# Forming the final row with tokens on partitions, in a one-layer decoder step

## The reference

```python
def rms_norm(x, g):
    return x * lax.rsqrt(jnp.mean(x * x, axis=-1, keepdims=True) + EPS) * g

def conv_ffn(h, buf, w_up, conv_w, conv_b, w_down):
    a, b = jnp.split(jnp.einsum('btd,de->bte', h, w_up), 2, axis=-1)
    a_ext = jnp.concatenate([buf, a], axis=1)
    c = conv_b + sum(conv_w[j] * a_ext[:, j:j + T] for j in range(3))
    y = jax.nn.gelu(c) * b
    return jnp.einsum('btf,fd->btd', y, w_down), a_ext[:, T:]

h = rms_norm(x, p['g_pre_ffn'])
y, new_buf = conv_ffn(h, conv_buf, p['w_up'], p['conv_w'], p['conv_b'], p['w_down'])
x = x + rms_norm(y, p['g_post_ffn'])
```

## Time and profile before

| | us |
|---|---|
| median of 3 runs | 2733.76 |
| lowest, highest run | 2732.91, 2734.69 |
| span of the profiled execution | 2732.5 |
| PE busy | 2686.0 |
| DVE busy | 1602.1 |
| ACT busy | 1075.3 |
| GpSimd (POOL) busy | 207.7 |

### The profile page before, as it was taken

One profiled execution on the slowest core, in us unless ns is written; L12 is line 12 of the kernel. 1 busy time (PEld: TensorE's weight loads), 2 busy tenths in 40 slices (PEclk: granted clock), 3 DMA queues, 4 the chain that ended last, 5 costly groups with the idle time before them and its releaser, 6 DMA issues.

```text
span 2732.5 us, 49450 instructions
## 1 busy us (share of the span) xinstructions
PE 2686.0 (98%) x20118; PEld 2555.5 (94%) x20118; DVE 1602.1 (59%) x2383; ACT 1075.3 (39%) x1357; POOL 207.7 (8%) x295
## 2 busy tenths in 40 slices
PE   8999999999999999999999999999999999999998
PEld 7999887899999999999989969999999999999997
DVE  5564564476777767777546334485655555653334
ACT  5333445444444444444333234342332233343324
POOL 0102311111111111111100000000000000000000
PEclk9999999999999999999999999999999999999999
DMA  9746656765555556555464694555555555555554
GB/s 268 206 124 164 214 169 209 225 192 157 155 141 159 154 149 163 141 159 154 132 200 130 223 385 110 144 167 149 154 146 146 153 150 144 142 139 150 153 151 146
DMA packets 693464, 458.69 MB, mean 168 GB/s; under 512 B 13646, under 2 KB 661422, under 8 KB 687342
## 3 DMA queue, kind: packets, MB, share of 16 engines
q1 hardware_dynamic: 681008, 414.25, 53.8%
q0 software_dynamic: 8608, 28.06, 3.6%
q10 hardware_dynamic: 3712, 14.35, 1.4%
HBM read 429.91 MB, written 26.72 MB: 167 GB/s over the span
## 4 chain that ended last, share of the span: by engine, by line
PE 93%; DVE 3%; DMA 2%; ACT 1%; issue 0%; SPq 0%; POOL 0%; DVEq 0%; ACTq 0%
PE psum L596 20%; PE psum L601 20%; PE psum L598 20%; PE psum L852 4%; PE psum L1284 4%; PE psum L1285 4%; PE psum L1286 4%; PE psum L857 2%; PE psum L994 1%; PE psum L997 1%; PE psum L990 1%; DMA ring<-in_w_in 1%; PE psum L1165 1%; PE psum L710 1%; PE psum L1006 1%; PE psum L1044 1%
## 5 line engine op out<-in xcount | busy, mean ns | idle before, releaser
L596 PE MATMUL psum<-x_high,w_high 128*128 128x320 f32 x3808 | 1123.8, 311 | 0.5 <-ACT w_high L2022 0.5
L598 PE MATMUL psum<-h_low,w_high 128*128 128x320 f32 x3312 | 974.3, 309 | 0.0
L1331 DVE TENSOR_TENSOR w_low<-ring,w_high 128x2048 fp32r<-128x2048 f32 x292 | 676.1, 2315 | 312.8 <-ACT w_high L2022 312.4
L2022 ACT ACTIVATE w_high<-ring 128x2048 fp32r<-128x2048 f32 x294 | 561.6, 1911 | 678.2 <-PE psum L601 554.9
L596 PEld LDWEIGHTS psum<-x_high,w_high 128*128 128x128 f32 x3808 | 713.0, 188 | 5.8 <-issue 2.4
L598 PEld LDWEIGHTS psum<-h_low,w_high 128*128 128x128 f32 x3312 | 621.9, 188 | 1.6
L601 PE MATMUL psum<-x_high,w_low 128*128 128x320 f32 x3808 | 597.4, 309 | 0.0
L601 PEld LDWEIGHTS psum<-x_high,w_low 128*128 128x128 f32 x3808 | 568.5, 188 | 0.0
L1284 PE MATMUL psum<-y_high,w_down_high 128*128 128x320 f32 x704 | 217.8, 309 | 1.2 <-DVE w_low L1941 1.2
L1286 PE MATMUL psum<-y_high,w_low 128*128 128x320 f32 x704 | 216.3, 307 | 0.0
L1285 PE MATMUL psum<-y_low,w_down_high 128*128 128x320 f32 x704 | 216.2, 307 | 0.0
(11 more groups left out here) (424 smaller groups left out, 2840.9 us busy)
## 6 DMA issues: line engine op xcount, KB each, us to landing
ring<-in_w_in SPq DMA_DIRECT2D x128, 1024.0 KB, 5.8
ring<-in_w_up SPq DMA_DIRECT2D x88, 1024.0 KB, 5.8
ring<-in_w_down SPq DMA_DIRECT2D x64, 704.0 KB, 4.8
ring<-in_w_xk SPq DMA_DIRECT2D x16, 1024.0 KB, 5.7
ring<-in_w_xv SPq DMA_DIRECT2D x16, 1024.0 KB, 5.0
ring<-in_w_out SPq DMA_DIRECT2D x16, 1024.0 KB, 6.0
ring<-in_w_xq SPq DMA_DIRECT2D x16, 1024.0 KB, 6.2
ring<-in_w_xo SPq DMA_DIRECT2D x16, 1024.0 KB, 6.0
```

The costliest lines, as they stand in the source:

```text
L596: mm(out, w_hi[:, j % 2, k, :], x_hi[:, k, :], start=k == 0, stop=False)
L598: mm(out, w_hi[:, j % 2, k, :], lo[:, k, :], start=False, stop=False)
L1331: V.tensor_tensor(w_lo[:, j], ring[:, j], w_hi[:, j % 2].bitcast(FP32), ALU.subtract).then_inc(N.slab_lo, 1)
L2022: F(w_hi[:, j % 2], ring[:, j], ACT.Copy).then_inc(N.slab_hi, 1)
```

## The change

- **x is turned early.** After each of the first two calls of `conv_gate`, DVE turns two chunks of x, all 32x32 blocks at once (`x_rows_turned`, four transposes of 128x1280), into the still empty end of `yT`. When all four are done ACT issues four DMAs that write x to DRAM as rows of tokens, in runs of 32 numbers (128 bytes), 5120 runs each. The parking by line 2686 goes. DVE waits for the four DMAs before its pass 6.
- **The convolution's columns** are turned by DVE in two transposes of 128x704 after two tiles of the down-projection; 16 GpSimd DMAs send them at once, in runs of 128 bytes. PE's and ACT's 11 groups in the tail go.
- **The tail.** SP fetches x as rows. PE turns the raw scaled `hT` without waiting for the root, three of twelve pieces ahead of the sums; the sums put one number per token on its partition (eight products with one column), so the root is 128x3. DVE does eight pieces in one operation each, h times root plus x, out of PSUM; ACT scales the four sample pieces and GpSimd adds them. ACT sends `y_sample` in one DMA.

```diff
...
             sp.wait_ge(N.slab_used, B_DOWN + R * (KD - 1) + 1)
-            sp.dma_start(xT, xt_dram).then_inc(N.x_fetched, 16)
-            sp.wait_ge(N.cn_evac, 11)
...
+            sp.wait_ge(N.x_parked, 16 * 4)
+            sp.dma_start(x_prompt, xr_dram[0:SEQ].rearrange("(m p) d -> p m d", p=P)).then_inc(N.x_fetched, 16)
+            sp.dma_start(x_sample, xr_dram[SEQ:T]).then_inc(N.x_fetched, 16)
             for q in range(4):
...
+                sp.wait_ge(N.xo_edve, 2 * q + 2)
+                sp.dma_start(O["y_prompt"][0].rearrange("(m p) d -> p m d", p=P)[:, :, c], x_prompt[:, :, c])\
                   .then_inc(N.final_sent, 16)
...
+            for u in range(3):
+                rows_out(u)
             pe.wait_ge(N.n_sum, 3)
...
+            pe.wait_ge(N.n_t, KD)
+            for b in (1, 2):
+                for m, r0, r1 in ((0, 0, P), (1, 0, P), (2, 0, NS), (2, NS, P)):
+                    t0 = TOK[m][0]
+                    last = mm(bank(b)[r0:r1, m:m + 1], sqacc[:, t0:t0 + r1 - r0], ones[:, 0:1], start=True, stop=True)
+                last.then_inc(N.n_mm, 1)
+            for u in range(3, 12):
+                rows_out(u)
...
+            def x_rows_turned(q):
+                dve.wait_ge(N.n_x, 8)
+                V.transpose(x_turned[:, q], chunk(xT, q)).then_inc(N.x_turned, 1)
...
             conv_gate(0, 0, False, first=(4,))
+            x_rows_turned(0)
+            x_rows_turned(1)
             conv_gate(0, 1, False, 6, 7, first=(5,))
+            x_rows_turned(2)
+            x_rows_turned(3)
...
             y_low(0, slice(0, DOWN_K))
+            dve.wait_ge(N.x_parked, 16 * 4)
             gates(6, FT // 2 - 7)
...
+            for half in range(2):
+                V.transpose(conv_turned[half], conv_window(half)).then_inc(N.conv_T, 1)
...
-            for q in range(4):
-                dve.wait_ge(N.n_t, 4 * q + 4)
-                st.then(V.tensor_tensor(chunk(hT, q), chunk(hT, q), bcast(rstd, 4), ALU.mult))
-                V.tensor_tensor(chunk(xT, q), chunk(xT, q), chunk(hT, q), ALU.add).then_inc(N.n_x, 1)
...
+            for u in OUT_DVE:
+                q, m = OUT_UNITS[u]
+                dve.wait_ge(N.xo_T, u + 1)
+                y = x_prompt[:, m, q * 512:(q + 1) * 512]
+                V.scalar_tensor_tensor(y, bank(OUT_BANKS[u % 6]), tok_root[:, m:m + 1], y, ALU.mult, ALU.add)\
+                    .then_inc(N.xo_edve, 1)
...
             conv_input(0, 1, False)
+            for i in range(4):
+                act.wait_ge(N.x_turned, 4)
+                act.dma_start(xr_dram.rearrange("(b t) (k i d) -> i t k b d", t=32, i=4, d=32)[i],
+                              x_turned[32 * i:32 * i + 32].rearrange("p q x -> p (q x)")
+                              .rearrange("p (k b d) -> p k b d", k=KD, d=32)).then_inc(N.x_parked, 16)
...
             inputs(1, 6)
-            act.wait_ge(N.x_parked, 16)
+            act.wait_ge(N.x_turned, 4)
...
+            for i, u in enumerate(OUT_ACT):
+                act.wait_ge(N.xo_T, u + 1)
+                F(y_part[:, i], bank(OUT_BANKS[u % 6])[0:NS], ACT.Copy, scale=tok_root[0:NS, 2:3]).then_inc(N.xo_eact, 1)
+            act.wait_ge(N.xo_pool, 4)
+            act.dma_start(O["y_sample"].rearrange("b t d -> (b t) d"), x_sample).then_inc(N.final_sent, 16)
...
-            pool.wait_ge(N.h_low, 2 * KD)
-            pool.wait_ge(N.n_sq, 10)
-            pool.dma_start(xt_dram, xT).then_inc(N.x_parked, 16)
...
+                for i in range(4):
+                    pool.dma_start(conv_prompt[i][:, f], conv_turned[half][32 * i:32 * i + 2]).then_inc(N.out_sent, 16)
+                    pool.dma_start(conv_sample[i][:, f], conv_turned[half][32 * i + 2:32 * i + 18]).then_inc(N.out_sent, 16)
+            pool.wait_ge(N.x_fetched, 32)
+            for i in range(4):
+                pool.wait_ge(N.xo_eact, i + 1)
+                y = x_sample[:, i * 512:(i + 1) * 512]
+                G.tensor_tensor(y, y, y_part[:, i], ALU.add).then_inc(N.xo_pool, 1)
```

More of the change, by code:

```diff
@@ L173, in hybrid_layer @@
         xt_dram = nc.dram_tensor("x_transposed", (P, KD, T), FP32, kind="Internal").ap()
+        xr_dram = nc.dram_tensor("x_rows_saved", (T, D), FP32, kind="Internal").ap()
         xh_dram = nc.dram_tensor("x_high_saved", (P, KD, T), FP32, kind="Internal").ap()
@@ L384, in hybrid_layer, with conv_window @@
         pcf = take(2, 4)
-        x_out = conv_rows
         assert top[0] <= SPLIT_AT
         top[0] = BASE
-        y_rows = take(3, D)
+        x_sample = take(D)[0:NS]
+        y_part = take(4, 512)[0:NS]
+        x_prompt = arena[:, X_AT:X_AT + 2 * D].rearrange("p (m d) -> p m d", m=2)
+        x_turned = yT[:, FT - KD:FT].rearrange("p k t -> p (k t)").rearrange("p (q x) -> p q x", q=4)
+        tok_root, tok_half, tok_tmp = small[:, 16:19], small[:, 24:27], small[:, 32:35]
+        def conv_window(half):
+            return bass.AP(tensor=conv_all.tensor, offset=conv_all.offset + half * (FT // 2) * 18,
+                           ap=[conv_all.ap[0], [18, FT // 2], [1, 32]])
         S = {n: sem(n) for n in """
@@ L445, in hybrid_layer @@
         Y_CUT, Y_PARTS = 6, (1, 2, 4, 5)
-        OUT_BANKS = (6, 7, 3, 0)
+        OUT_BANKS = (3, 4, 5, 6, 7, 0)
+        OUT_UNITS = [(q, m) for q in range(3) for m in range(3)] + [(3, 2), (3, 0), (3, 1)]
+        OUT_DVE = [u for u, (q, m) in enumerate(OUT_UNITS) if m < 2]
+        OUT_ACT = [u for u, (q, m) in enumerate(OUT_UNITS) if m == 2]
         ATT_S = float(P) ** -0.5
@@ L1288, in _, with rows_out @@
                         last.then_inc(N.slab_used, 1)
-            pe.wait_ge(N.n_sum, 3)
[L1290 to L1307, removed]
+            def rows_out(u):
+                q, m = OUT_UNITS[u]
+                t0, rows = TOK[m]
+                pe.wait_ge(N.n_t, 4 * q + 4)
+                if u == 5:
+                    pe.wait_ge(N.bank_free, B_DOWN + KD - 1 + FREE)
+                if u >= 6 and u - 6 in OUT_DVE:
+                    pe.wait_ge(N.xo_edve, OUT_DVE.index(u - 6) + 1)
+                elif u >= 6:
+                    pe.wait_ge(N.xo_eact, OUT_ACT.index(u - 6) + 1)
+                for c in range(4):
+                    last = tr(bank(OUT_BANKS[u % 6])[0:rows, c * P:(c + 1) * P], hT[:, 4 * q + c, t0:t0 + rows], ident)
+                last.then_inc(N.xo_T, 1)
+            for u in range(3):
+                rows_out(u)
+            pe.wait_ge(N.n_sum, 3)
+            pe.wait_ge(N.n_t, KD)
[6 more added lines that the diff above has]
+                rows_out(u)
         @block.vector
@@ L1960, in down_tile @@
                     down_low(it, e, j)
-                if not last:
-                    down_low(it, e + 1, 0)
+                if last:
+                    dve.wait_ge(N.n_sq, 11)
+                    V.tensor_tensor(sqacc, sqacc, sqbuf[:, 1], ALU.add).then_inc(N.n_sum, 1)
+                    return
+                down_low(it, e + 1, 0)
                 y = hT[:, ds(it * 2 + e, 1)].rearrange("p o t -> p (o t)")
@@ L2542, in down_tile @@
                 met()
+                if last:
+                    F(sqbuf[:, 1], bank(e)[:, 0:T], ACT.Square).then_inc(N.n_sq, 1)
+                    F(hT[:, KD - 1], bank(e)[:, 0:T], ACT.Copy, scale=G_POST_FFN[:, KD - 1:KD]).then_inc(N.n_t, 1)
+                    return
                 F(hT[:, ds(it * 2 + e, 1)].rearrange("p o t -> p (o t)"), bank(e)[:, 0:T], ACT.Copy).then_inc(N.bank_free, 1)
@@ L2551, in _ @@
             down_tile(KD // 2 - 1, 1, True)
[L2552 to L2562, removed]
+            act.wait_ge(N.n_mm, 7)
+            st.then(F(tok_root, bank(1)[:, 0:3], ACT.Ln, scale=1.0 / D, bias=small[:, 63:64]))
+            F(tok_root, tok_root, ACT.Exp, scale=-0.5).then_inc(N.n_seed, 1)
+            act.wait_ge(N.n_var, 6)
+            for i, u in enumerate(OUT_ACT):
[3 more added lines that the diff above has]
+            act.dma_start(O["y_sample"].rearrange("b t d -> (b t) d"), x_sample).then_inc(N.final_sent, 16)
         @block.gpsimd
@@ L2694, in _ @@
                                   conv_old[:, f, :].rearrange("p o (b t) -> p (o b) t", t=2)).then_inc(N.ctx_ready, 1)
-            pool.wait_ge(N.out_sent, 96)
+            conv_prompt = O["new_conv_prompt"][0, 0].rearrange("c (f i d) -> i c f d", i=4, d=32)
+            conv_sample = O["new_conv_sample"][0].rearrange("b j (f i d) -> i (b j) f d", i=4, d=32)
+            for half in range(2):
+                f = slice(half * (FT // 2), (half + 1) * (FT // 2))
+                pool.wait_ge(N.conv_T, half + 2)
+                for i in range(4):
[6 more added lines that the diff above has]
+                G.tensor_tensor(y, y, y_part[:, i], ALU.add).then_inc(N.xo_pool, 1)
+            pool.wait_ge(N.out_sent, 96 + 16 * 16)
             pool.wait_ge(N.state_sent, 32 * NHG)
```

36 lines of the change are left out of this document (18 added, 18 removed).

## The result

After the change the kernel takes 2749.09 us (median of 4 runs, 2748.18 to 2751.44), beside 2733.34 us of the kernel before, run beside it (4 runs). The ratio is 1.0056, with a 95% interval of 1.0044 to 1.0068: slower by 15.8 us, where +18.1 was forecast. The profiled execution has a span of 2747.6 us, 15.1 more than before. All medians and ratios here leave out two executions of the kernel before, run beside the last experiments, that took 3281 and 4905 us at a mean granted clock of 0.75 and 0.82.

The account below looks back on a forecast made before the run. PE was taken as the bound, busy 2686.0 of 2732.5 us. Terms -9.6 + 24.9 + 2.8 = +18.1 us gave a span of 2750.6, a median (1.3 above) of 2751.9 us; range 2729 to 2772.

Parts of the forecast that it names:

- PE's idle time at tile 6: Start of the up-projection: PE waits from 1820.65 to 1845.5 us for ACT's `w_high`, 24.9 us.
- the hold: ACT's queue before `w_high` of tile 6: four DMA issues keep ACT from 1821.0 to 1843.5 us, three behind another DMA.
- The clock: Tile 6 after PE's idle time: granted clock falls to 0.50, 24 products take 6.2 instead of 3.4 us, cost 2.8 us.
- The tail: From the last product to the end: the new tail gives 9.6 us, bounds 7.5 to 11.5.
- The eight products with one column: Sums of squares in the tail: no row shows one, taken as 1.5 us, nearer the upper bound of 2.1.
- Covered work: `w_low` of tile 5 ready 0.5 us before PE wants it; convolution columns' DMAs and transposes run beside the down-projection.
- Cost: nothing: Down-projection: the convolution columns' 16 DMAs and two transposes cost nothing there, 1.8 us if that cover is gone.
- Short issues: ACT's queue takes four large DMAs at 0.4 us each, PE idles 4.0 us: 2728.2 or 2731.0 us; chance 0.20.
- Dear writes of 28 to 50 ns: Short DRAM writes at that time a packet: ACT held 26.9 to 48 us, total 2761 to 2783 us; chance 0.15.
- Hidden: Start of tile 6: PE's wait is hidden after all, the whole 9.6 us stays, 2724.2 us; chance 0.05.
- Transposes at half rate: DVE's four transposes of x take twice 1.41 us each: 5.6 us later, 2757.5 us; no chance of its own, inside the range.
- about 3: Hold of ACT in all, in us, at which the forecast decides between faster and slower.

Follow-up runs that it names:

- the room of 32: The changed kernel with 32 instead of 24 words of room behind the saved convolution columns: 2748.03 us, ratio 1.0054 to the kernel before.

## Why the prediction was right

The sign, the mechanism and its place were right: 2751.9 us forecast, 2749.1 measured. Step by step:

- **PE's idle time at tile 6**: 24.9 us forecast, 20.5 measured. The transposes ended as forecast (1820.95 against 1821.1), and with them the wait that is left without DMAs (2.6 us). The term that was mis-sized is the hold, 22.5 us (0.4 + 1.2 + 17.3 + 3.6) against 17.87. I took 18 ns a packet, 17.3 us for three DMAs; from 1825.65 to 1839.02 us 15231 packets passed on 16 engines, 14.0 ns each, 13.4 us. The 1.2 us to the first packet and the 3.6 us of the weight load were two terms of the sum; measured, they are one stretch of 3.8 us before the first packet, in which 1819 of the load's packets passed. With 0.7 for the first issue that makes 17.9. Where the DMAs stood apart the first packet also came 2.8 to 3.5 us after the end of its issue, again with a load's packets in between, so how much of the 3.8 us is the load's is not shown.
- **The clock**: 2.8 forecast, 2.3 measured.
- **The tail**: 9.6 forecast, 10.1 measured. Less the shift of 25.2 us, the root is ready at 2711.2 (2711.7 forecast), and the last store of `y_prompt` is issued at 2716.6 (2717.2). The eight products with one column, the most uncertain term, took 1.47 us against 1.5; DVE's eight operations 5.36 against 5.5.
- **Covered work**: the `w_low` of tile 5 was ready at 1817.75, 0.5 us before PE wanted it, as forecast. Of the convolution's columns no cost shows on PE beyond, at most, the 0.4 us of the down-projection that stay open: the two transposes took 0.87 and 0.92 us beside the down-projection.
- **What was missing**: 2.3 us in the down-projection. "Cost: nothing" was true of the work that moves there, and not of the room that it needs. I had costed the instructions of the edit and not the addresses that it shifts. That the total came within 3 us is in part luck: this was hidden by the errors the other way, (24.9 - 20.5) + (2.8 - 2.3) + (10.1 - 9.6) = 5.4 us; the difference of the two is the 3 us by which the forecast was high.
- **Rivals.** Short issues: out, the second to fourth took 5.0 to 6.8 us. Dear writes of 28 to 50 ns: out, 14.1. Hidden: out. Transposes at half rate: out, 1.47 to 1.51 us each. By the prediction's own terms the two signs meet at a hold of 9.6 - 2.8 - 2.4 = 4.4 us and not at "about 3"; with the measured terms it is 10.1 - 2.3 - 2.3 - 2.6 = 2.9 us, so that figure came out right by luck.

The Trainium skill ("DMA: Bandwidth & Descriptors", Issuing engines are not separate DMA queues) says that issuing from another engine saves only the time to initiate a DMA, usually small relative to the DMA. Here an issue took up to 6.8 us, of DMAs that landed 9.5 to 13.2 us after they were issued, so it was not small. The same page of the Trainium skill (Specifications) says that below 512 B the DMA engine reads, modifies and writes. That did not make these stores dear in the sense of the rival: 14.1 ns, close to the 13.4 of the packets of 64 and 256 bytes in the earlier trace rows.

## What to carry to other kernels

Count the runs of a DMA, not only its bytes, and look at what stands behind the second one on the engine that issues it: that instruction waited here until most of the first one's packets had passed. DMAs of many short runs are cheap one at a time on an engine with slack, and dear in a row ahead of work that a bottleneck waits for. An edit that shifts a buffer can change the speed of the products that read it, so compare the mean time of one product by group, before and after (of groups that alternate, their sum), even in stages that were not touched.

## What was not expected of the hardware

- A product that reads the same data at another address took up to 3 ns more, 307 to 310 ns with 320 columns. Over the 64 slabs this is about 2 us. Shown: it goes with the address both ways, when `y_high1` to `y_high3` and what lies behind them move. Open: which addresses are good. With all operands on multiples of 64 the 48 slabs took 231.0 us. With `y_high1` to `y_high3` on such multiples and the rest 32 bytes past, they took 231.1 us in the kernel before and 232.4 us with the room of 32.
- Four DMAs of 32 runs each (20 KB a run) still held ACT for 4.96 us, up to 2.3 us an issue, while few of their packets had passed.
- After 2.6 us without work PE found a granted clock of 0.52, and its tile took 1.8 us longer.
- Writes to DRAM in runs of 128 bytes went at 145 GB/s, 14.1 ns a packet on each DMA engine.
